# Out projection, feed-forward, norm and the second attention's first head joined without barriers, and the last feed-forward pair run piece by piece

## The chip, the cores and the metric

The kernel runs on one core of a Trainium2 chip. The metric is the device time of one execution in microseconds (us), lower is better. The times given are medians over runs.

## What is computed

One inference step of an encoder with two layers, for 1024 prompt tokens and 32 new ones, all in fp32. Layer 0 mixes tokens by sparse attention (a small indexer picks 256 keys per query), layer 1 by differential attention with 8 heads. Behind each mixer stand an out projection, a residual and a norm, and behind these the feed-forward part, a gated per-layer embedding and a second norm:

```python
    yp = layer_norm(ALPHA * yp + mp, ln_gain[i, 0], ln_bias[i, 0])     # mp = mixer's output @ w_out

def channel_and_ple(x, p, w13, w2, w_ple, w_gate, g, b):
    gate, up = jnp.split(x @ w13, 2, axis=-1)
    ffn = (jax.nn.silu(gate) * up) @ w2
    ple = jax.nn.sigmoid(x @ w_gate) * (p @ w_ple)
    return layer_norm(ALPHA * x + ffn + ple, g, b)
```

Model width is 1024, the feed-forward part's 2816, the embedding's 256. Outputs are the rows of both token sets after layer 1, and each layer's new keys and values.

## The kernel before

**Products.** An fp32 matrix is kept as two fp32r parts, high (rounded) and low (the rest), and a product is three matmuls: high by high, high by low, low by high. The tokens stand as columns: `x_hi` and `x_lo` hold the layer's input (128 partitions x 8 x 1056), `o_col` the running sum. The 1056 tokens are cut into three pieces of 352 for products with columns, or into nine tiles (eight of 128 and one of 32) for out projections and norms. A unit is a weight block of 8 x 128 x 128 (or 2 x 128 x 128 for the embedding), and its product with one piece is 24 matmuls of 352 columns (`unit_product`, `product`), in one PSUM bank.

**The ring.** SP loads a unit into `w_raw[s]` (`load_unit`, once the slot's previous unit is split), POOL splits it into `w_hi[s]` and `w_lo[s]` (`split_unit`, two operations, once TensorE has finished with the slot), TensorE waits for the split (`unit_ready`). There are four slots; `ring_plan` lists which slot each unit of a phase uses. A feed-forward pass uses 0, 1, 0, 1, 2, 3.

**Phases.** `program` runs ten: `load_x`, `index_projection`, `mixer_a`, `out_norm` A, `ffn` 0, `norm_tokens` 0, `attention_b`, `out_norm` B, `ffn` 1, `norm_tokens` 1. Each gives one function per engine. TensorE, ACT and DVE end every phase with a drain and wait for one another on `phase_over`; SP and POOL wait for that count only where a phase says so:

```python
                eng.drain().then_inc(c.phase_over, 1)
                eng.wait_ge(c.phase_over, 3 * n + 3)
```

Within a phase the order on each engine is the order in which its function is written; semaphores join them.

**`out_norm`** goes tile by tile. TensorE turns the mixer's output (B only, `turn_o`), multiplies it by the out weights (48 matmuls of 512 columns, line 1522) and, after six of the eight units, turns back the normalised rows of the tile before (`turn_back`). ACT makes `o_hi` (`o_high`, line 1537), DVE `o_lo` (line 1583). DVE adds the residual and takes statistics, ACT the root, DVE the coefficients, ACT the normalised rows `y_rows` (line 1566), and from the turned rows `x_new` (line 1574), which POOL splits into `x_hi` and `x_lo`. `o_hi` of tile t+1 is issued in the loop's turn of tile t, at its start.

**`ffn`** first loads p, turns it (line 1847) and splits it; then come eight columns of the gated embedding (a gate unit with sigmoid, a projection unit), and 11 passes of a hardware loop. Each pass, a *pair*, has two gate units, two up units, each for three pieces, silu and the product `h`, and then for each piece eight down products of 6 matmuls (line 1901), which DVE adds to `o_col` (line 1987).

**`norm_tokens`** turns `o_col` tile by tile into rows (line 1702), normalises them (root line 1736, rows line 1742), multiplies by the gain (POOL line 1692 in layer 0, DVE line 1760 in layer 1), adds the shift on POOL (line 1694) and stores them; in layer 0 it also turns them back and splits them (lines 1712, 1727, 1752). **`attention_b`** begins with the projections of its first head: V, K and Q units by three pieces each, with turns of V's and K's rows between.

Of the kernel before, what the change touches and what calls it, by code (L numbers as in the profile page):

```python
# [6 lines left out]
ALU = mybir.AluOpType  # L7
# [10 lines left out]
PIECES = 3  # L18
TP = TOK // PIECES
# [57 lines left out]
def ring_plan():  # L77

    phases = [("index", 1, [0, 1, 0, 1, 0]), ("attnA", 6, [0, 1]), ("outA", 1, [0, 1]),
              ("ple0", KC // 2, [0, 1, 2, 3]), ("ffn0", DFF // P // 2, [0, 1, 0, 1, 2, 3]),  # L80
              ("attnB", BH // 2, [0, 1, 0, 1, 0, 1]), ("outB", 1, [0, 1]),
              ("ple1", KC // 2, [0, 1, 2, 3]), ("ffn1", DFF // P // 2, [0, 1, 0, 1, 2, 3])]
    base, plan = [0] * 4, {}
    for name, passes, slots in phases:
        plan[name] = (tuple(base), slots)
        for s in range(4):
            base[s] += passes * slots.count(s)
# [82 lines left out]
def load_x(c):  # L170
# [27 lines left out]
    def pool(g):  # L198
# [793 lines left out]
def attention_b(c):  # L992
# [20 lines left out]
    squares = place("squares", [P, P], BF16)  # L1013
    assert at <= SAMPLE_OUT
# [10 lines left out]
    no = c.phase_no  # L1025
# [6 lines left out]
    FIRST_BANKS = (6, 0, 1, 2, 3, 6, 0, 1, 6)  # L1032
# [31 lines left out]

    def sync(sp):
        def weights(h, u):
            at = ((2 * D, D, 0)[u]) + P * h
            load_unit(c, sp, name, *unit(h, u), [(whole, w[:, :, at:at + P])], KC)

        for u in (V, K, Q):  # L1070
            weights(0, u)
        sp.wait_ge(c.phase_over, 3 * no)
        for h in range(BH):
# [6 lines left out]
            if h + 1 < BH:  # L1080
                weights(h + 1, V)
# [3 lines left out]
            if h + 1 < BH:  # L1085
                weights(h + 1, K)
# [3 lines left out]
            if h + 1 < BH:  # L1090
                weights(h + 1, Q)
# [16 lines left out]
    def tensor(pe):  # L1108
        def bank_read(h, n):
# [6 lines left out]
        def project(h, u, t):  # L1116
# [3 lines left out]
            before = [x for x in range(n) if piece_bank(h, x // 3, x % 3) == b]  # L1120
            if before:
                bank_read(h, before[-1])
            elif h >= 1:
                bank_read(h - 1, 8)
            last = unit_product(c, bank(c, b, TP), s, KC, c.x_hi, c.x_lo, t)
            piece_done(c, last, t, s_piece, s)

        def turn_rows(h, r):
            pe.wait_ge(s_col, 6 * h + (2, 3, 3, 5, 6, 6)[r])
            if 6 * h + r >= 1:  # L1130
                pe.wait_ge(s_rows, 6 * h + r)
            b = bank(c, ROWS)
            for j, t in enumerate(row_tiles(r)):
                cols = P if t < QT else NEW
                mm = nc.tensor.transpose(b[0:cols, P * j:P * j + P], col[:, P * t:P * t + cols], c.ident[:, :])
# [54 lines left out]
        for step in items(0):  # L1190
            for what in step:
                item(0, what)
# [13 lines left out]
    def scalar(act):  # L1206
        def project(h, u, t):
            i, v = unit(h, u)
            await_piece(c, act, name, i, v, t, s_piece, 3 * h + u)
# [57 lines left out]
        for step in items(0):  # L1267
            for what in step:
                item(0, what)
# [13 lines left out]
    def vector(v):  # L1283
        def project(h, u, t):
# [4 lines left out]
            if u == K:  # L1289
                v.wait_ge(s_col, 6 * h + 3 + t + 1)  # L1290
# [50 lines left out]

        v.wait_ge(s_iota, 2)
# [5 lines left out]
        for step in items(0):  # L1348
            for what in step:
                item(0, what)  # L1350
# [16 lines left out]
def out_norm(c, kind):  # L1367
# [87 lines left out]
    def pool(g):  # L1455
# [11 lines left out]
        for t in range(T):  # L1467
# [649 lines left out]
```

## Time and profile before

| what | us |
|---|---|
| median of 3 runs | 3404.48 (3397.68 to 3405.16) |
| profiled execution | 3402.7 |
| its span in the trace | 3400.9 |
| TensorE busy | 3134.8 (92%) |
| POOL, DVE, ACT busy | 1042.6, 1513.2, 887.1 |
| mean granted clock of TensorE | 0.952 of full |

All phases run one after the other on one core. Busy shares are over the whole span; the profile also gives them for any stretch, with the clock that was granted to TensorE in it (1.00 is full, 2.4 GHz). The chain that ended last leads back from the last instruction through whatever released each one. In a timeline row the bracket gives how long the engine was idle before and what ended that.

### The profile page before, as it was taken

The page shows a single profiled execution, that of the slowest core. Times are in us where ns is not written, and L with a number is a line of the kernel's source. Part 1 is how long each engine was busy: PE and PEld are TensorE (multiplying, and loading weights), DVE is VectorE, ACT ScalarE, POOL GpSimd, SP SyncE. Part 2 cuts the span into 40 slices and gives each one's busy share as a digit, 9 for nine tenths or more (in the row PEclk, how much of TensorE's full clock was granted, in tenths as well). Part 3 has the DMA queues.
Part 4 walks back from the last instruction along what each step waited for, and adds up shares of the span by engine and source line. Part 5 has one row for each costly group of instructions (what it writes and reads, how often), then busy time and mean ns, then how long its engine had stood idle before and what let it go on. Part 6 is the DMA issues. An engine that isn't in the chain of part 4 may idle for free.

```text
span 3400.9 us, 49928 instructions
## 1 busy us (share of the span) xinstructions
PE 3134.8 (92%) x19621; PEld 2921.1 (86%) x19621; DVE 1513.2 (44%) x2880; ACT 887.1 (26%) x1921; POOL 1042.6 (31%) x504
## 2 busy tenths in 40 slices
PE   7896999976999999999968999987889999999996
PEld 7586777764999999999967999976689999999996
DVE  2589764432434333432352555563334343334335
ACT  2355444423110111101122445453311101110112
POOL 2132000032443334333443222213244433443333
PEclk8998799988999999999988999998989999999997
DMA  2121000011211111111112111111021111111111
GB/s 82 32 51 51 1 1 1 1 56 36 65 45 62 37 43 43 55 44 43 44 47 68 55 41 46 47 39 56 21 75 50 44 56 37 44 48 56 37 49 51
DMA packets 209355, 149.48 MB, mean 44 GB/s; under 512 B 28914, under 2 KB 195764, under 8 KB 209236
## 3 DMA queue, kind: packets, MB, share of 16 engines
q1 hardware_dynamic: 209236, 147.85, 14.2%
q8 instruction: 80, 1.31, 0.2%
q14 instruction: 39, 0.32, 0.0%
HBM read 128.09 MB, written 19.73 MB: 43 GB/s over the span
## 4 chain that ended last, share of the span: by engine, by line
PE 84%; DVE 7%; ACT 3%; issue 2%; POOL 1%; DMA 1%; ACTq 0%; SPq 0%; POOLq 0%; DVEq 0%
PE psum L151 46%; PE psum L1901 15%; PE psum L1522 5%; PE psum L612 4%; PE psum L578 2%; PE psum L593 2%; DVE junk L827 2%; PE psum L1186 2%; PE psum L1160 2%; PE psum L1174 1%; PE psum L533 1%; PE psum L547 1%; ACT x_newA L1574 1%; DVE ln_part L1769 1%; ACT x_newB L1574 1%
## 5 line engine op out<-in xcount | busy, mean ns | idle before, releaser
L151 PE MATMUL psum<-x_hi,w_hi 128*128 128x352 f32 (+1 forms) x3192 | 1040.6, 326 | 29.5 <-POOL w_lo L122 13.8
L151 PE MATMUL psum<-x_lo,w_hi 128*128 128x352 f32 (+1 forms) x3192 | 1028.1, 322 | 0.0
L151 PE MATMUL psum<-x_hi,w_lo 128*128 128x352 f32 (+1 forms) x3192 | 1028.0, 322 | 0.0
L120 POOL TENSOR_TENSOR w_hi<-w_raw,zeros 128x1024 fp32r<-128x1024 f32 (+1 forms) x209 | 386.8, 1851 | 1615.4 <-PE psum L151 1359.2
L151 PEld LDWEIGHTS psum<-x_hi,w_hi 128*128 128x128 f32 (+1 forms) x3192 | 601.8, 189 | 31.6 <-issue 21.2
L151 PEld LDWEIGHTS psum<-x_lo,w_hi 128*128 128x128 f32 (+1 forms) x3192 | 602.9, 189 | 0.4
L151 PEld LDWEIGHTS psum<-x_hi,w_lo 128*128 128x128 f32 (+1 forms) x3192 | 601.6, 188 | 0.5
L122 POOL TENSOR_TENSOR w_lo<-w_raw,w_hi 128x1024 fp32r<-128x1024 f32 (+1 forms) x209 | 485.1, 2321 | 16.4
L1973 DVE TENSOR_TENSOR gate<-psum,gate 128x352 f32<-128x352 f32 x132 | 69.3, 525 | 830.5 <-PE psum L151 830.5
L1901 PE MATMUL psum<-h_hi,w_hi 128*128 128x352 f32 x1056 | 340.6, 323 | 0.0
L1901 PE MATMUL psum<-h_lo,w_hi 128*128 128x352 f32 x1056 | 338.3, 320 | 0.0
L1901 PE MATMUL psum<-h_hi,w_lo 128*128 128x352 f32 x1056 | 338.0, 320 | 0.0
L1987 DVE TENSOR_TENSOR o_col<-psum,o_col 128x352 f32<-128x352 f32 x528 | 263.4, 519 | 149.3 <-PE psum L1901 147.1
L1977 DVE TENSOR_TENSOR h_lo<-gate,h_hi 128x352 fp32r<-128x352 f32 x132 | 210.2, 1617 | 0.3
L1901 PEld LDWEIGHTS psum<-h_lo,w_hi 128*128 128x128 f32 x1056 | 198.4, 188 | 0.0
L1901 PEld LDWEIGHTS psum<-h_hi,w_hi 128*128 128x128 f32 x1056 | 198.0, 188 | 0.0
L1901 PEld LDWEIGHTS psum<-h_hi,w_lo 128*128 128x128 f32 x1056 | 197.9, 187 | 0.0
L1933 ACT ACTIVATE h_hi<-gate 128x352 fp32r<-128x352 f32 x132 | 65.8, 498 | 469.6 <-DVE gate L1973 469.6
L612 PEld LDWEIGHTS psum<-valsA,ptA 128*128 128x128 f32 (+1 forms) x1216 | 150.2, 194 | 37.6 <-issue 21.4
L612 PE MATMUL psum<-valsA,ptA 128*128 128x65 f32 (+1 forms) x1216 | 168.3, 283 | 0.9 <-ACT ptA L698 0.4
L1930 ACT ACT_TABLE_LOAD x22 | 28.2, 1283 | 532.7 <-PE psum L151 532.7
L1327 DVE CUSTOM_DVE_ANT_0 probB<-psum,distB 128x128 f32<-128x128 f32 (+5 forms) x144 | 96.4, 707 | 121.5 <-PE psum L1160 120.5
(458 smaller groups left out, 4166.9 us busy)
## 6 DMA issues: line engine op xcount, KB each, us to landing
w_raw<-in_ffn_w_dram SPq DMA_DIRECT2D x132, 512.0 KB
w_raw<-in_b_w_in_dram SPq DMA_DIRECT2D x24, 512.0 KB
w_raw<-in_ple_w_gate_dram SPq DMA_DIRECT2D x16, 512.0 KB
x_nat<-in_x_prompt_dram SPq DMA_DIRECT2D x8, 512.0 KB, 3.7
w_raw<-in_a_w_in_dram SPq DMA_DIRECT2D x8, 512.0 KB
w_raw<-in_a_w_in_dram SPq DMA_DIRECT2D x16, 256.0 KB
x_rows<-x_rows SPq DMA_DIRECT2D x8, 512.0 KB, 2.6
out_new_b_v_prompt_dram<-valsB SPq DMA_DIRECT2D x8, 512.0 KB, 3.4
```

The lines of the kernel that those rows point to most:

```text
L120: nc.gpsimd.tensor_tensor(c.w_hi[s][:, 0:kc], c.w_raw[s][:, 0:kc], zero, ALU.add).then_inc(c.split[s], 1)
L122: nc.gpsimd.tensor_tensor(c.w_lo[s][:, 0:kc], c.w_raw[s][:, 0:kc], c.w_hi[s][:, 0:kc].bitcast(F32), ALU.subtract).then_inc(c.split[s], 1)
L151: last = c.nc.tensor.matmul(out, w, x, start=(n == 0), stop=(n == 3 * len(terms) - 1))
L578: mm = nc.tensor.matmul(c.psum[0:n, 1024 * m + a:1024 * m + a + size], queries[rows, 4 * c2 + 2 * i + j, q:q + n], keys[rows, c2, key:key ...
L593: mm = nc.tensor.transpose(bank(c, 4 + k % 2)[0:size, P * x:P * x + n], prob[0:n, g % 3, m, key:key + size], c.ident[0:n, 0:n])
L612: mm = nc.tensor.matmul(c.psum[0:n, at:at + 65], pt[0:size, k, x, 0:n], vals[0:size, blk, 2 * c2 + m, :], start=(j == 0 and x == 0), stop= ...
L1327: nc.vector.tensor_tensor_reduce(prob[:, sl, m, 0:L], c.psum[:, 1024 * m:1024 * m + L], dist[:, o:o + L], slope(h), -LOWEST, ALU.add, ALU.min,
L1522: mm = nc.tensor.matmul(out, o[t % 2][:, u, 0:n], ww[:, cols], start=(j == 0 and x == 0), stop=(j == KC - 1 and x == 2))
L1901: mm = nc.tensor.matmul(o, w[s][:, m, :], h[:, j, piece(t)], start=(j == 0 and k == 0), stop=(j == 1 and k == 2))
L1973: nc.vector.tensor_tensor(gate[:, 1, piece(t)], bank(c, 3 + t, TP), gate[:, 0, piece(t)], ALU.mult).then_inc(s_h, 1)
L1977: nc.vector.tensor_tensor(h_lo[:, j, piece(done)], gate[:, 1, piece(done)], h_hi[:, j, piece(done)].bitcast(F32), ALU.subtract).then_inc(s ...
L1987: nc.vector.tensor_tensor(o, bank(c, (6 + m) % 8, TP), o, ALU.add).then_inc(s_da, 1)
```

## The change

1. **Ring.** Six slots; each of the six units of a feed-forward pair has its own. Slots 4 and 5 lie where p and its two parts lay, whose last use is before the first pair.
2. **Out projection.** `o_hi` and `o_lo` are issued two tiles ahead, from the turn of tile t for tile t+2. The last tile's turn back is given to the next phase.
3. **From out projection to feed-forward.** No barrier. SP loads the first two embedding units before p, POOL splits them in the out projection's loop after tile 6, TensorE runs the first gate unit's pieces 0 and 1 right after the last tile's product, then the last turn back, the turns of p, and piece 2.
4. **`ffn` and `norm_tokens` become `ffn_norm`.** The loop has 10 passes; the last pair is written out piece by piece, and the turns of the norm stand between its pieces. The gain is now multiplied on DVE in both layers.
5. **Norm and first head.** In layer 0 the norm's later tiles (turns of 5 to 8, turns back of 4 to 8) are issued between the V, K and Q pieces of `attention_b`'s first head. V's and K's weights are loaded and split before the third tile's shift.
6. Barriers stay behind `load_x`, `index_projection`, `mixer_a`, `attention_b` and at the end.

The core of the diff:

```diff
@@ ring_plan @@
-              ("ple0", KC // 2, [0, 1, 2, 3]), ("ffn0", DFF // P // 2, [0, 1, 0, 1, 2, 3]),
+              ("ple0", KC // 2, [0, 1, 2, 3]), ("ffn0", DFF // P // 2, [0, 1, 2, 3, 4, 5]),
@@ out_norm, pool @@
+            if t == T - 3:
+                c.ple_first[layer](g)
@@ out_norm, tensor @@
-        turn_back(T - 1)
@@ out_norm, scalar @@
-            if t >= 1 and t + 1 < T:
-                o_high(t + 1)
+            if t + 2 < T:
+                o_high(t + 2)
             act.wait_ge(s_mv, b_mv + t + 1)
@@ out_norm, vector: after the coefficients of tile t @@
-            if t >= 1 and t + 1 < T:
-                o_low(t + 1)
...
+            if t + 2 < T:
+                o_low(t + 2)
@@ ffn_norm, sync @@
+        ple_unit(sp, 0, 0)
+        ple_unit(sp, 0, 1)
+        sp.wait_ge(s_omm, b_o + T)
         sp.dma_start(p_nat[:, 0:QT, :], c.dram["p_prompt"][layer, 0].rearrange("(t p) n -> p t n", p=P)).then_inc(s_pn, 16)
@@ ffn_norm, pool @@
+        for u in range(6):
+            split_unit(c, g, fn, L, u, KC)
+        g.wait_ge(s_par, b_par + 32)
+        shifted(g, 0)
+        shifted(g, 1)
+        if not last_one:
+            split_unit(c, g, "attnB", 0, 0, KC)
+            split_unit(c, g, "attnB", 0, 1, KC)
+        for t in range(2, T):
+            shifted(g, t)
@@ ffn_norm, tensor @@
+        gate_input(0, 0)
+        gate_input(0, 1)
+        c.turn_back_last[layer](pe)
+        pe.wait_ge(s_oy, 2 * b_o + 2 * T)
+        turn_p()
+        gate_input(0, 2)
+        turn_p_sample()
...
+        gate_last(0, 0)
+        up_last(0, 0)
+        gate_last(1, 0)
+        up_last(1, 0)
+        gate_last(0, 1)
+        down_last(0)
+        turn_rows(pe, 0)
+        up_last(0, 1)
+        turn_rows(pe, 1)
+        gate_last(1, 1)
+        if not last_one:
+            turn_back(pe, 0)
+        up_last(1, 1)
+        if not last_one:
+            turn_back(pe, 1)
+        gate_last(0, 2)
+        down_last(1)
+        turn_rows(pe, 2)
+        up_last(0, 2)
+        turn_rows(pe, 3)
+        gate_last(1, 2)
+        if not last_one:
+            turn_back(pe, 2)
+        up_last(1, 2)
+        turn_rows(pe, 4)
+        if not last_one:
+            turn_back(pe, 3)
+        down_last(2)
+        if last_one:
+            for t in range(5, T):
+                turn_rows(pe, t)
@@ attention_b, tensor @@
+        late.turn(pe, 5)
+        late.turn(pe, 6)
+        late.back(pe, 4)
+        project(0, V, 0)
+        late.turn(pe, 7)
+        late.back(pe, 5)
+        project(0, K, 0)
+        late.back(pe, 6)
+        late.turn(pe, 8)
+        project(0, V, 1)
+        late.back(pe, 7)
+        project(0, K, 1)
+        late.back(pe, 8)
+        project(0, V, 2)
+        project(0, K, 2)
+        turn_rows(0, 0)
+        project(0, Q, 0)
...
@@ program @@
-        for make, *args in ((load_x,), (index_projection,), (mixer_a,), (out_norm, "A"),
-                            (ffn, 0), (norm_tokens, 0), (attention_b,), (out_norm, "B"), (ffn, 1),
-                            (norm_tokens, 1))[:LIMIT]:
+        for make, *args in ((load_x,), (index_projection,), (mixer_a,), (out_norm, "A"), (ffn_norm, 0), (attention_b,),
+                            (out_norm, "B"), (ffn_norm, 1))[:LIMIT]:
+            goes_on = make is out_norm or (make is ffn_norm and args[0] == 0)
```

The functions `turn_rows`, `stats`, `root`, `coefs`, `normal`, `gained`, `shifted`, `turn_back`, `high` and `low` of `ffn_norm` hold the same instructions as `norm_tokens` did, one tile each.

**ACT in the first out projection.** Here `o_hi0A` and `o_hi1A` are the two buffers of `o_hi`, the line with `ln_coefA` is the root, the one with `y_rows` the normalised rows. Before, from the last of the weights on:

```order
L1548 ACTIVATE far_hi5A<-w_raw 128x1024
L1564 ACT_TABLE_LOAD
L1564 ACTIVATE ln_coefA<-ln_mvA,eps 128x1
L1566 ACTIVATE y_rows0A<-y_rows0A,ln_coefA 128x1024
L1574 ACTIVATE x_newA<-psum,params 128x128 x8
L1537 ACTIVATE o_hi0A<-o_col 128x1024
L1564 ACTIVATE ln_coefA<-ln_mvA,eps 128x1
L1566 ACTIVATE y_rows1A<-y_rows1A,ln_coefA 128x1024
L1574 ACTIVATE x_newA<-psum,params 128x128 x8
L1537 ACTIVATE o_hi1A<-o_col 128x1024
```

And now:

```order
L1662 ACTIVATE far_hi5A<-w_raw 128x1024
L1651 ACTIVATE o_hi0A<-o_col 128x1024
L1678 ACT_TABLE_LOAD
L1678 ACTIVATE ln_coefA<-ln_mvA,eps 128x1
L1680 ACTIVATE y_rows0A<-y_rows0A,ln_coefA 128x1024
L1688 ACTIVATE x_newA<-psum,params 128x128 x8
L1651 ACTIVATE o_hi1A<-o_col 128x1024
L1678 ACTIVATE ln_coefA<-ln_mvA,eps 128x1
L1680 ACTIVATE y_rows1A<-y_rows1A,ln_coefA 128x1024
L1688 ACTIVATE x_newA<-psum,params 128x128 x8
```

`o_hi` of tile 2 stood behind `x_new` of tile 0 and now stands ahead of tile 0's root; so for every later tile.

**ACT in the last pair of layer 0.** From the silu of the second third's first gate (`gate_130`) on; L2194 is silu, L2198 makes `h_hi`, L1863 is the root, L1880 the normalised rows, L1897 `x_hi` of the next layer. None of the norm's rows stood here before:

```order
L2194 ACTIVATE gate_130<-psum 128x352
L1863 ACT_TABLE_LOAD
L1863 ACTIVATE ln_coef_138<-ln_mv_137,eps 128x1
L1880 ACTIVATE x_rows_0_131<-psum,ln_coef_138 128x1024
L2198 ACTIVATE h_hi_128<-gate_130 128x352
L1863 ACTIVATE ln_coef_138<-ln_mv_137,eps 128x1
L1880 ACTIVATE x_rows_0_132<-psum,ln_coef_138 128x1024
L2194 ACT_TABLE_LOAD
L2194 ACTIVATE gate_130<-psum 128x352
L1897 ACTIVATE x_hi<-psum 128x4x128 x2
```

The norm of tiles 0 and 1 now stands between two silus, with a table load on each side.

**POOL after the last pair of layer 0.** Before, the V and K splits (L120, L122) stood behind all nine gains (L1692) and shifts (L1694); the last rows of the norm and what followed were:

```order
L1692 TENSOR_TENSOR x_rows_0_127<-x_rows_0_127,gain_rows_128 32x1024
L1694 TENSOR_TENSOR x_rows_0_127<-x_rows_0_127,shift_rows_129 32x1024
L120 TENSOR_TENSOR w_hi<-w_raw,zeros 128x1024
L122 TENSOR_TENSOR w_lo<-w_raw,w_hi 128x1024
L120 TENSOR_TENSOR w_hi<-w_raw,zeros 128x1024
L122 TENSOR_TENSOR w_lo<-w_raw,w_hi 128x1024
L1099 IOTA distB 128x1024
```

And now (L1891 is the shift, L121 and L123 the split):

```order
L1891 TENSOR_TENSOR x_rows_0_131<-x_rows_0_131,shift_rows_135 128x1024
L1891 TENSOR_TENSOR x_rows_0_132<-x_rows_0_132,shift_rows_135 128x1024
L121 TENSOR_TENSOR w_hi<-w_raw,zeros 128x1024
L123 TENSOR_TENSOR w_lo<-w_raw,w_hi 128x1024
L121 TENSOR_TENSOR w_hi<-w_raw,zeros 128x1024
L123 TENSOR_TENSOR w_lo<-w_raw,w_hi 128x1024
L1891 TENSOR_TENSOR x_rows_0_133<-x_rows_0_133,shift_rows_135 128x1024
```

The gains are gone from POOL, and the two splits stand between the shifts of tiles 1 and 2.

## Rows read from the trace of the kernel before

**Rows 1.** The page: busy us by engine; the chain that ended last.

```profile
PE 3134.8 (92%) x19621; PEld 2921.1 (86%) x19621; DVE 1513.2 (44%) x2880; ACT 887.1 (26%) x1921; POOL 1042.6 (31%) x504
...
PE psum L151 46%; PE psum L1901 15%; PE psum L1522 5%; PE psum L612 4%; PE psum L578 2%; PE psum L593 2%; DVE junk L827 2%; PE psum L1186 2%; PE psum L1160 2%; PE psum L1174 1%; PE psum L533 1%; PE psum L547 1%; ACT x_newA L1574 1%; DVE ln_part L1769 1%; ACT x_newB L1574 1%
```

**Rows 2.** Busy time by stretch: us, PE, PEld, DVE, ACT, POOL busy (x count), PEclk, DMA, GB/s.

```profile
707.03:821.80 114.77, 92.48 (x394) 73.95 (x392) 34.97 (x57) 37.07 (x77) 33.00 (x14) 0.93 0.09 29
...
722.29:737.67 15.38, 12.08 (x57) 9.76 (x57) 5.00 (x9) 5.39 (x11) 5.16 (x3) 1.00 0.10 34
...
821.80:835.50 13.70, 13.70 (x56) 6.56 (x56) 2.87 (x7) 4.25 (x10) 2.20 (x1) 0.88 0.01 1
...
835.50:856.90 21.40, 4.66 (x27) 4.26 (x26) 6.88 (x12) 6.44 (x16) 9.90 (x7) 0.68 0.41 112
...
856.93:860.40 3.47, 3.47 (x13) 3.47 (x14) 0.00 (x0) 0.00 (x0) 3.31 (x4) 0.54 0.61 178
...
2332.02:2448.32 116.30, 97.31 (x441) 79.93 (x439) 35.62 (x69) 38.57 (x84) 26.67 (x13) 0.91 0.09 29
...
2460.50:2482.00 21.50, 5.07 (x27) 4.51 (x27) 6.99 (x12) 6.47 (x16) 9.95 (x7) 0.60 0.40 111
...
976.30:1733.60 757.30, 757.30 (x4752) 757.04 (x4752) 267.13 (x397) 77.72 (x143) 279.82 (x128) 1.00 0.14 43
...
1733.60:1839.75 106.15, 64.62 (x381) 60.36 (x380) 38.18 (x76) 29.07 (x51) 60.31 (x28) 0.79 0.23 77
...
3358.50:3400.90 42.40, 15.16 (x73) 11.61 (x72) 30.67 (x55) 14.77 (x19) 21.11 (x9) 0.59 0.26 103
```

**Rows 3.** Timeline, out projection tiles: start us, us, engine, line, tiles [idle before it].

```profile
751.41 1.09 ACT L1537 ACTIVATE o_hi0A<-o_col 128x1024 fp32r<-128x1024 f32 x1
...
752.53 2.07 DVE L1583 TENSOR_TENSOR o_lo0A<-o_col,o_hi0A 128x1024 fp32r<-128x1024 f32 x1 [11.56 <-ACT o_hi0A L1537]
...
754.66 0.69 PE L1522 MATMUL psum<-w_hi,o_hi0A 128*128 128x512 f32 x1 [3.29 <-DVE o_lo0A L1583]
...
765.65 2.90 ACT L1574 ACTIVATE x_newA<-psum,params 128x128 f32<-128x128 f32 x8 [6.41 <-PE psum L1501]
...
2407.68 1.03 PE L1501 MATMUL psum<-ident,y_rows0B 128*128 128x128 f32 x8
```

**Rows 4.** The chain of waits, second out projection: start us, us, what, count.

```profile
2332.02 8.21 PE psum L1522 x36
```

**Rows 5.** Timeline between first out projection and feed-forward phase.

```profile
841.41 1.06 PE L1501 MATMUL psum<-ident,y_rows0A 32*128 32x32 f32 x8 [5.89 <-ACT y_rows0A L1566]
...
844.90 0.39 SPq L1818 DMA_DIRECT2D p_nat<-in_p_prompt_dram  x1
...
850.88 3.34 PE L1847 MATMUL psum<-ident,p_nat 128*128 128x128 f32 x16 [8.41 <-DMA p_nat<-in_p_sample_dram]
```

**Rows 6.** Timeline of the first norm phase.

```profile
1734.30 1.97 PE L1702 MATMUL psum<-ident,o_col 128*128 128x128 f32 x16 [0.67 <-DVEq L2068]
...
1737.12 1.28 ACT L1736 ACT_TABLE_LOAD   x1 [25.12 <-DVE ln_mv L1773]
...
1739.13 1.20 ACT L1742 ACTIVATE x_rows<-psum,ln_coef 128x1024 f32<-128x1024 f32 x1 [0.42 <-DVE ln_coef L1777]
...
1741.10 1.74 DVE L1777 SCALAR_TENSOR_TENSOR ln_coef<-ln_mv,ln_coef 128x1 f32<-128x1 f32 x1
...
1742.90 2.34 POOL L1694 TENSOR_TENSOR x_rows<-x_rows,shift_rows 128x1024 f32<-128x1024 f32 x1
...
1747.31 1.08 ACT L1727 ACTIVATE x_hi<-psum 128x512 fp32r<-128x512 f32 x2 [0.80 <-PE psum L1712]
...
1748.42 1.29 DVE L1752 TENSOR_TENSOR x_lo<-psum,x_hi 128x512 fp32r<-128x512 f32 x2 [3.17 <-ACT x_hi L1727]
```

**Rows 7.** Timeline of the last norm phase.

```profile
3366.14 1.22 DVE L1760 TENSOR_TENSOR x_rows<-x_rows,gain_rows 128x1024 f32<-128x1024 f32 x1
...
3374.74 0.48 PE L1702 MATMUL psum<-ident,o_col 128*128 128x128 f32 x1 [1.61 <-ACT x_rows L1742]
```

More of the change, by code:

```diff
@@ L1347, in vector @@
         v.wait_ge(s_dist, 2)
-        for step in items(0):
-            for what in step:
-                item(0, what)
+        project(0, Q, 0)
+        rows(0, 3)
+        project(0, Q, 1)
+        rows(0, 4)
+        project(0, Q, 2)
+        rows(0, 5)
+        late.rows_stored(v)
         for g in range(STEPS + 2):
@@ new lines, in gained, with shifted, high @@
+    def gained(v, t):
+        n = rows(t)
+        v.wait_ge(s_n, b_n + t + 1)
+        nc.vector.tensor_tensor(xt[t % 3][0:n, :], xt[t % 3][0:n, :], gain[0:n, :], ALU.mult).then_inc(s_gn, 1)
+    def shifted(g, t):
+        n = rows(t)
+        g.wait_ge(s_gn, b_gn + t + 1)
+        nc.gpsimd.tensor_tensor(xt[t % 3][0:n, :], xt[t % 3][0:n, :], shift[0:n, :], ALU.add).then_inc(s_x, 1)
+    def high(act, t):
+        n = rows(t)
+        act.wait_ge(s_bt, t + 1)
+        for b in (0, 1):
+            ins = nc.scalar.activation(c.x_hi[:, 4 * b:4 * b + 4, tokens(t)],
+                                       bank(c, 4 + b).rearrange("p (k q) -> p k q", k=4)[:, :, 0:n], ACT.Copy)
+        ins.then_inc(s_hi, 1)
@@ new lines, in low, with rows_stored @@
+    def low(v, t):
+        n = rows(t)
+        v.wait_ge(s_hi, t + 1)
+        for b in (0, 1):
+            ins = nc.vector.tensor_tensor(c.x_lo[:, 4 * b:4 * b + 4, tokens(t)],
+                                          bank(c, 4 + b).rearrange("p (k q) -> p k q", k=4)[:, :, 0:n],
+                                          c.x_hi[:, 4 * b:4 * b + 4, tokens(t)].bitcast(F32), ALU.subtract)
+        ins.then_inc(s_lo, 1)
+    def rows_stored(eng):
+        for j in range(3):
+            eng.wait_ge(s_out[j], b_out + 48)
@@ new lines, in high_last @@
+        def high_last(j, t):
+            act.wait_ge(s_h, b_h + 3 + last_count(j, t))
+            nc.scalar.activation(h_hi[:, j, piece(t)], gate[:, 1, piece(t)], ACT.Copy).then_inc(s_hh, 1)
+        silu_last(0, 0)
+        high_last(0, 0)
+        silu_last(1, 0)
+        high_last(1, 0)
+        silu_last(0, 1)
+        root(act, 0)
+        normal(act, 0)
+        high_last(0, 1)
+        root(act, 1)
+        normal(act, 1)
+        silu_last(1, 1)
+        if not last_one:
+            high(act, 0)
```

832 lines of the change are left out of this document (534 added, 298 removed).

## The prediction

> **What bounds the kernel now.** I read the page first: TensorE is busy for 3134.8 us of the span of 3400.9, and the chain that ended last is made of its products, with single percents for DVE and ACT lines [rows 1]. So a change pays where TensorE waits or runs slowly, and the next view is busy time by stretch. The steady part needs no help: ten and a bit of the eleven feed-forward pairs show 757.30 us of TensorE in 757.30, at clock 1.00 [rows 2]. The change touches the other rows of that view: the two loops of the out projection (92.48 busy of 114.77, and 97.31 of 116.30), the stretches from an out projection to its feed-forward (21.40 and 21.50 us, with 4.66 and 5.07 busy), the first norm with the second attention's first head (64.62 of 106.15), and the last norm (15.16 of 42.40) [rows 2]. Their idle time and low clocks hold all that can be won. The timeline then tells what each wait is.
>
> Unit prices, all from rows: a matmul of 352 columns at full clock takes 757.30 / 4752 = 0.159 us, so a piece of 24 takes 3.82 and a down piece of 48 takes 7.63 [rows 2]; one of 512 takes 8.21 / 36 = 0.228 [rows 4]; eight transposes take 1.03 [rows 3]. A pair takes 12 pieces of 3.82 and three of 7.63, 68.7 us.
>
> **The change, part by part.** The sum is made against the profiled execution, 3402.7 us, which is 1.8 above its span and 1.8 below the median of the runs.
>
> *Out projection, loop.* Before each tile TensorE waits 3.29 us for o_lo, which DVE began at once when ACT's o_hi was there; o_hi stood behind the previous tile's x_new of 2.90 us on ACT's queue [rows 3]. The change issues o_hi and o_lo two tiles ahead, so both are done about a tile before use. They take 1.09 and 2.07 us [rows 3], and neither engine is full: ACT 37.07 and DVE 34.97 of 114.77 [rows 2]. What is late next is nothing: a tile's normalised rows are turned after six of eight units of the next tile's products, and I see no wait there. A tile then takes 48 x 0.228 + 1.03 = 11.98 us; its busy time was 12.08 in the one tile shown, at clock 1.00 [rows 2]. Seven tiles: 83.9 for 114.77, **-30.9**. The short last tile goes from 13.70 at clock 0.88 to 12.0, **-1.7** [rows 2]. In the second one a tile has another eight transposes: 13.0, so 91 for 116.30, **-25.3**.
>
> *From out projection to feed-forward.* Of 21.40 us TensorE works 4.66 [rows 2]. It waits 5.89 for the last tile's rows, then the barrier, then the DMAs of p, issued at 844.90, after which its transposes start at 850.88 [rows 5]. The change loads the first gate weights before p, splits them on POOL during tile 6, and puts two gate pieces (2 x 3.82) right behind the last product: they cover the 5.89. The DMA of p is issued when the last product ends, and had taken 850.88 - 844.90 = 6.0 us, less than the 7.6 of the pieces. What is left is 1.06 + 3.34 of transposes [rows 5], some 0.3 for p's sample, and 0.5 for odd waits, an estimate: 5.2 for 21.40, **-16.2**. The pieces themselves are only moved. At the old start 13 matmuls took 3.47 us at clock 0.54, where 13 x 0.159 = 2.07 [rows 2]; without the idle stretch ahead that goes: **-1.7** with its neighbours. The second boundary: 21.50 to 5.2, and the same 1.7, **-18.0**.
>
> *Six-slot ring.* Each of the six units of a pair has its own slot. POOL's work stays the same (279.82 us for 64 units, 4.37 each, in 757.30) [rows 2], TensorE had no wait there, so **0**. Its cover is that a unit's split is needed a pair later; the last rival says what it costs if that goes.
>
> *Last pair of layer 0, norm, first head.* Before: 68.7, and 106.15 to the first logits [rows 2]: 174.8. After, the pair is cut by pieces, and the turns of tiles 0 to 4 and back-turns of 0 to 3 stand between them. Pair 68.7, nine groups of transposes 9.3. Waits: a tile's chain from the end of its turn (1734.30, of which half the 16, so 1735.3) over the table load of 1.28 to the end of its normalised rows (1739.13 + 1.20) is 5.0 us [rows 6]. The next turn needs this tile's bank and comes behind one piece of 3.82, so it waits 1.2, at tiles 1 and 3; 0.7 ahead of tiles 0 and 2, as for the first turn now [rows 6], for the last add. POOL splits V and K weights (two units, 8.7 us) between the shifts of tiles 1 and 2. K's slot comes free after the second up piece of the last third; 4.37 of split and 2.34 of shift [rows 6] make 6.7 us, the back-turn of tile 2 comes 1.2 + 1.03 + 3.82 = 6.0 later: 0.7. A DVE operation on one element lasted 1.74 us there and ended as POOL's did [rows 6]; for such holdings I add 1.8 to that wait and 1.2 at the adds. Together 7.5 of waits, pair 85.5. From there nine groups of transposes (9.3), nine pieces (34.4), row turns (2.6), 46.3, and 0.7 first. The waits here stand on chains with no piece of the right length beside them: a back-turn is followed by x_hi 1.08 and x_lo 1.29 [rows 6], before which a product may not start. I take 8, from 9 back-turn chains of which most have a piece in between. Bounds: 0 if all is covered, and 25 if each of nine tiles shows its 1.08 + 1.29 plus 0.4. Total 140.5 for 174.8, **-34.3**, within -42 and -17.
>
> Moved past on the queues: SP issues gain, shift and the V and K loads ahead of the stores of the rows, Q's among them; V and K wait for slots whose own splits the pair's first pieces have needed. On POOL, Q's split (4.37) waits for V's last piece and runs against K's last piece and a row turn, 3.82 + 0.5: even, 0. The stores end beside products, the iotas too.
>
> DVE now multiplies by gain in layer 0 too, 1.22 us a tile [rows 7], POOL only shifts: in stretches where TensorE's pieces are the longer path, 0.
>
> A table load cost 1.28 us here, and the normalised rows, with the root and two DVE operations in between, began 0.73 us after its end (1738.40 to 1739.13) [rows 6]. *ScalarE: Activation LUTs* of the Trainium skill, section "What ACT_TABLE_LOAD costs", puts a switch at about 2.66 us, a drain included. Behind this load the trace has no room for one. By the page the four switches in the open, at tiles 0 and 2 of both layers, would each add 1.4, and the sum would end 5.5 us higher.
>
> *Last norm.* Five of nine turns go into the last pair: 5.1 of transposes and 5.4 of waits by the same chain, 10.5 more there. What is left runs as before from tile 5's turn at 3374.74 to the end at 3400.9, 26.2 us [rows 7]. 42.40 becomes 36.6, **-5.8**.
>
> Sum: 30.9 + 1.7 + 17.9 + 25.3 + 18.0 + 34.3 + 5.8 = 133.9. 3402.7 - 133.9 = 3268.8, and with 1.8 to the median **3271 us**.
>
> **Rivals.**
> 1. *The clock falls among the turns.* For: the stretch with the norm has mean clock 0.79, those at the boundaries 0.68 and 0.60, the last norm 0.59 [rows 2], each with waits and transposes. Against: the tile from 722.29 ran eight transposes in its twelve busy microseconds at 1.00 after waits of 3.3 us [rows 2, 3]. If the late part (55 us) and 30 us of the two last pairs run at 0.8, that adds 85 x 0.25, 21 less some waiting it hides: about 16, 3287. The Trainium skill's *TensorE: Matmul & The Clock Gate*, "Part 4: PE-mode transpose", says that a transpose does not count as PE-busy in the same way; by it the fall would come wherever turns stand close together, which is this rival. The tile at 1.00 speaks against it only where products surround the turns.
> 2. *Longer chains.* ACT and DVE run one written order through pieces, norm and splits; each waits for the other and for POOL, and one late operation shifts all. If half the 34.3 and the 5.8 is lost: +20, 3291.
> 3. *The out projection has another bound.* The chain product, add, statistics, root, rows, turn, x_new, POOL's split might need more than a tile. At 15 us a tile the 14 full tiles give back 14 x 2.5 to 3.0, 40: 3311. Against: no engine but TensorE has over a third of that stretch [rows 2].
> 4. *The ring turns serial, slower.* Had the order of slots been wrong, so that POOL may split a unit only when the pair ahead has ended, each of 20 steady pairs would show a split of 4.37 and a load of 512 KB, at the 178 GB/s of [rows 2] 2.9 us: 7.3 us, 146 in all, 3417. It decides from 6.7 us a pair. Against: the first slot is free after 11.4 us of a pair of 68.7, and the last two are wanted 45.8 us into the next.
> 5. *The work joined does nothing*, since the waits come back at the first product that needs the same data: about 3400. The rows name causes that the change does remove, so little for this.
>
> **How the numbers follow.** The forecast has 0.66, on its own 3254 to 3285 (-8 and +17 in the head, and a few for each boundary). Rival 1 has 0.13, rival 2 0.10, rival 3 0.05, rival 4 0.03, rival 5 0.03. The range 3252 to 3304 takes in the first two rivals and leaves out the others and both tails, under 2 in 10. A change of 0.2% is 6.8 us, about what a measurement can tell. Faster by more: 0.66 + 0.13 + 0.10 + 0.05, and half of rival 5, 0.95; same 0.02; slower 0.03.
>
> **What would show it.** In the profile after: tiles of 12.0 and 13.0 us in the out projections, with o_hi ahead of the root and no wait for o_lo; about 5 us of TensorE time outside products between last tile and gate, clock near 1.00 at its first pieces; 68.7 us for a steady pair, with no wait for a split; the last pair of layer 0 at about 85 us, waits of about 1.2 us at the turns of tiles 1 and 3; first logits 140 us after the last pair's start. I am wrong if a tile takes over 13.5 us, if TensorE waits in a steady pair, or if the granted clock of the last pair or the first head falls below 0.9.

## The result and the profile after

The changed kernel takes 3288.4 us (median of 4 runs, 3282.6 to 3293.85) where the kernel before takes 3404.6 beside it; the ratio is 0.9666 (95% interval 0.9655 to 0.9678). That is 116 us less. The forecast was 3271, 134 less, with a range of 3252 to 3304.

The page of the changed kernel, busy time and the chain that ended last, answering to [rows 1] (L152 is the product, L2033 the down product, L1637 the out projection):

```profile
PE 3108.2 (94%) x19621; PEld 2902.7 (88%) x19621; DVE 1554.4 (47%) x2889; ACT 887.2 (27%) x1921; POOL 1021.8 (31%) x495
...
PE psum L152 48%; PE psum L2033 15%; PE psum L1637 6%; PE psum L613 5%; PE psum L579 3%; PE psum L594 3%; DVE junk L828 2%; PE psum L1225 2%; PE psum L1199 2%; PE psum L1213 1%; PE psum L534 1%; PE psum L548 1%; PE psum L1174 0%; PE psum L1591 0%; DMA x_nat<-in_x_prompt_dram 0%
```

Busy time by stretch, columns as in [rows 2]. The ten rows are: seven tiles of the first out projection, its last tile, the way through the third gate piece, the wait at the feed-forward part, ten pairs, the last pair, the rest of the norm with the first head to its first logits, seven tiles of the second out projection, the second boundary, and the last norm.

```profile
711.72:794.50 82.78, 82.78 (x393) 69.15 (x394) 35.31 (x56) 35.62 (x70) 25.77 (x12) 1.00 0.12 39
797.40:809.21 11.81, 11.81 (x57) 6.16 (x56) 4.08 (x7) 4.31 (x11) 9.86 (x6) 1.00 0.11 34
809.21:827.36 18.15, 16.11 (x100) 15.38 (x98) 6.65 (x11) 8.04 (x18) 11.29 (x9) 0.91 0.50 137
930.60:942.41 11.81, 0.21 (x2) 0.00 (x0) 11.58 (x7) 0.00 (x0) 11.65 (x6) 0.70 0.31 89
942.41:1630.85 688.44, 688.44 (x4321) 688.44 (x4322) 244.77 (x359) 70.64 (x130) 256.17 (x119) 1.00 0.15 44
1630.85:1716.20 85.35, 79.72 (x505) 77.51 (x504) 42.08 (x75) 23.84 (x35) 29.92 (x13) 0.98 0.06 26
1716.20:1774.50 58.30, 49.03 (x309) 46.72 (x309) 25.26 (x43) 16.53 (x33) 20.25 (x11) 0.94 0.25 77
2263.21:2352.27 89.06, 89.06 (x449) 74.60 (x450) 43.37 (x69) 36.45 (x76) 25.76 (x12) 1.00 0.11 36
2366.98:2383.57 16.59, 14.54 (x100) 13.82 (x98) 6.65 (x11) 8.04 (x18) 9.86 (x6) 1.00 0.51 145
3263.43:3292.07 28.64, 5.51 (x33) 4.05 (x32) 16.48 (x25) 5.69 (x8) 9.35 (x4) 0.62 0.20 78
```

TensorE works through both loops without a wait, at full clock, and a pair takes 68.84 us, as was said. One row was in no term of the sum: 11.8 us in which TensorE does nothing, in front of the first feed-forward product. To see what each part gave, both traces are cut at the same products (start times of matmuls, in us):

| stretch | before | after | difference | forecast |
|---|---|---|---|---|
| start to first out product of layer 0 | 688.3 | 697.4 | +9.1 | 0 |
| first to last product, out projection, layer 0 | 146.9 | 111.4 | -35.4 | -32.6 |
| to the last embedding product | 138.1 | 121.7 | -16.4 | -17.9 |
| to the first feed-forward product | 3.0 | 11.9 | **+8.9** | 0 |
| to the first logits of the second attention | 863.5 | 832.0 | -31.4 | -34.3 |
| to the first out product of layer 1 | 477.6 | 477.5 | -0.1 | 0 |
| first to last product, out projection, layer 1 | 142.8 | 114.6 | -28.1 | -25.3 |
| to the last embedding product | 138.2 | 120.1 | -18.1 | -18.0 |
| to the first feed-forward product | 3.0 | 11.9 | **+8.9** | 0 |
| to the end | 799.6 | 793.5 | -6.2 | -5.8 |

The first row is code that the change does not touch. Over the fourteen traces of this study it lies between 684.6 and 697.4. Without it the difference is -117.9, and the forecast's -133.9 with the two new waits added is -116.1.

The timeline of the changed kernel ahead of that product, DVE, POOL and TensorE (start us, us; the bracket is the idle time before and its end):

```profile
932.81 0.51 DVE L2267 TENSOR_TENSOR gate<-psum,gate 128x352 f32<-128x352 f32 x1
933.36 1.67 DVE L2270 SCALAR_TENSOR_TENSOR o_col<-x_lo,gate 128x352 f32<-128x352 f32 x1
934.72 2.50 POOL L123 TENSOR_TENSOR w_lo<-w_raw,w_hi 128x1024 fp32r<-128x1024 f32 x1
935.06 2.54 DVE L2273 SCALAR_TENSOR_TENSOR o_col<-x_hi,o_col 128x352 f32<-128x352 f32 x1
937.18 2.17 POOL L121 TENSOR_TENSOR w_hi<-w_raw,zeros 128x1024 fp32r<-128x1024 f32 x1
937.52 0.51 DVE L2267 TENSOR_TENSOR gate<-psum,gate 128x352 f32<-128x352 f32 x1
938.07 1.67 DVE L2270 SCALAR_TENSOR_TENSOR o_col<-x_lo,gate 128x352 f32<-128x352 f32 x1
939.43 2.50 POOL L123 TENSOR_TENSOR w_lo<-w_raw,w_hi 128x1024 fp32r<-128x1024 f32 x1
939.77 2.55 DVE L2273 SCALAR_TENSOR_TENSOR o_col<-x_hi,o_col 128x352 f32<-128x352 f32 x1
942.41 0.66 PE L152 MATMUL psum<-x_hi,w_hi 128*128 128x352 f32 x1 [11.60 <-ACTq L2176]
```

A piece's three DVE operations take 4.7 us, and the two with both inputs in SBUF end just after an operation of POOL; the one with an input in PSUM takes 0.51 beside POOL all the same. POOL is splitting the first pair's third unit and those behind it, which in four slots could not start before the pair did: in the trace of the kernel before, POOL's last split ahead of the pair ends at 965.74, DVE's last nine operations come from 971.76 on, and each lasts 0.52 or 0.53. And the signal that TensorE waited for is ACT's, which the change had moved behind DVE's last addition. The theory: the six slots let POOL into DVE's way, and the moved signals put the whole DVE chain in front of TensorE. By opening signals I mean the `sem_inc` calls with which ACT and DVE say, before the first pair, that its banks and buffers are free; in the kernel before both gave them ahead of the embedding's loop.

### The profile page after: what moved, and what is told of

Its sections match the earlier page's. It is cut to its first block, busy times and chain, and to the rows that moved or that the text cites. A ratio compares the mean times of both kernels' runs of the same rounds, so it can differ in the third digit from the quotient of the medians.

```text
span 3292.1 us, 49272 instructions
## 1 busy us (share of the span) xinstructions
PE 3108.2 (94%) x19621; PEld 2902.7 (88%) x19621; DVE 1554.4 (47%) x2889; ACT 887.2 (27%) x1921; POOL 1021.8 (31%) x495
## 4 chain that ended last, share of the span: by engine, by line
PE 88%; DVE 6%; issue 2%; ACT 2%; POOL 1%; DMA 1%; POOLq 0%; SPq 0%; ACTq 0%; DVEq 0%
PE psum L152 48%; PE psum L2033 15%; PE psum L1637 6%; PE psum L613 5%; PE psum L579 3%; PE psum L594 3%; DVE junk L828 2%; PE psum L1225 2%; PE psum L1199 2%; PE psum L1213 1%; PE psum L534 1%; PE psum L548 1%; PE psum L1174 0%; PE psum L1591 0%; DMA x_nat<-in_x_prompt_dram 0%
## 5 line engine op out<-in xcount | busy, mean ns | idle before, releaser
L152 PE MATMUL psum<-x_hi,w_hi 128*128 128x352 f32 (+1 forms) x3192 | 1041.4, 326 | 40.1 <-ACTq L2176 23.2
L152 PE MATMUL psum<-x_lo,w_hi 128*128 128x352 f32 (+1 forms) x3192 | 1028.0, 322 | 0.0
L152 PE MATMUL psum<-x_hi,w_lo 128*128 128x352 f32 (+1 forms) x3192 | 1027.9, 322 | 0.0
L121 POOL TENSOR_TENSOR w_hi<-w_raw,zeros 128x1024 fp32r<-128x1024 f32 (+1 forms) x209 | 381.9, 1827 | 1549.6 <-PE psum L152 957.8
L152 PEld LDWEIGHTS psum<-x_hi,w_hi 128*128 128x128 f32 (+1 forms) x3192 | 601.7, 189 | 42.8 <-ACTq L2176 23.8
L152 PEld LDWEIGHTS psum<-x_lo,w_hi 128*128 128x128 f32 (+1 forms) x3192 | 602.8, 189 | 0.5
L152 PEld LDWEIGHTS psum<-x_hi,w_lo 128*128 128x128 f32 (+1 forms) x3192 | 601.5, 188 | 0.5
L123 POOL TENSOR_TENSOR w_lo<-w_raw,w_hi 128x1024 fp32r<-128x1024 f32 (+1 forms) x209 | 491.8, 2353 | 16.4
L2033 PE MATMUL psum<-h_hi,w_hi 128*128 128x352 f32 x1056 | 340.8, 323 | 1.3 <-DVE h_lo L2308 1.0
L2033 PE MATMUL psum<-h_lo,w_hi 128*128 128x352 f32 x1056 | 338.3, 320 | 0.0
L2033 PE MATMUL psum<-h_hi,w_lo 128*128 128x352 f32 x1056 | 338.1, 320 | 0.0
L2033 PEld LDWEIGHTS psum<-h_hi,w_hi 128*128 128x128 f32 x1056 | 198.0, 188 | 2.0 <-issue 1.6
L2033 PEld LDWEIGHTS psum<-h_lo,w_hi 128*128 128x128 f32 x1056 | 198.3, 188 | 0.0
L2033 PEld LDWEIGHTS psum<-h_hi,w_lo 128*128 128x128 f32 x1056 | 197.9, 187 | 0.0
L2290 DVE TENSOR_TENSOR h_lo<-gate,h_hi 128x352 fp32r<-128x352 f32 x120 | 197.3, 1670 | 0.0
```

The costliest lines, as they stand in the source:

```text
L121: nc.gpsimd.tensor_tensor(c.w_hi[s][:, 0:kc], c.w_raw[s][:, 0:kc], zero, ALU.add).then_inc(c.split[s], 1)
L123: nc.gpsimd.tensor_tensor(c.w_lo[s][:, 0:kc], c.w_raw[s][:, 0:kc], c.w_hi[s][:, 0:kc].bitcast(F32), ALU.subtract).then_inc(c.split[s], 1)
L152: last = c.nc.tensor.matmul(out, w, x, start=(n == 0), stop=(n == 3 * len(terms) - 1))
L2033: mm = nc.tensor.matmul(o, w[s][:, m, :], h[:, j, piece(t)], start=(j == 0 and k == 0), stop=(j == 1 and k == 2))
L2290: nc.vector.tensor_tensor(h_lo[:, j, piece(done)], gate[:, 1, piece(done)], h_hi[:, j, piece(done)].bitcast(F32), ALU.subtract).then_inc(s ...
```

## The experiments

Times are medians beside runs of the kernel before on the same chip. "Wait" is the stretch from the last embedding product to the first feed-forward product in the run's trace (layer 0, layer 1), where the changed kernel has 11.9 and 11.9 and the kernel before 3.0 and 3.0.

### The wait in front of the feed-forward part

**ACT's signal early.**

```diff
+        act.sem_inc(s_si, 3)
         for x in range(4):
             p_high(x)
...
         act.wait_ge(s_acc, b_acc + 3 * KC)
-        act.sem_inc(s_si, 3)
```

> The changed kernel with one line moved: ACT gives its three opening signals for the feed-forward gates (s_si) before the embedding part, as the kernel before did, and no longer after DVE's last addition. Theory: the wait of 11.60 us at the first feed-forward product of each layer is for that signal; without it TensorE waits only for DVE's last gate multiply, which ended at 938.03 where the product started at 942.41, so the wait becomes about 7.5 us, 4 less in each layer, 8 us less in all. Rival (the wait has another cause, such as a split that comes late): the wait stays at 11.6 and the time stays.

3285.1 us, ratio 0.9658 (0.9645 to 0.9672); waits 10.0 and 9.6. The wait now ends with a signal of DVE (9.7 us, DVEq L2277), for which the change has the same order: its opening `sem_inc` calls stand behind the last addition too. So only 2 us went in each layer, half of what was expected, and the median's 3 us lie inside the interval. ACT's signal was the last of several, not the only one.

**POOL held back.**

```diff
         with g.Fori(0, L) as i:
             for u in range(6):
+                if u == 2:
+                    g.wait_ge(s_acc, b_acc + 3 * KC)
                 split_unit(c, g, fn, i, u, KC)
```

> The changed kernel with one wait added: POOL splits the third unit of the first feed-forward pair only after DVE's last addition of the embedding part. Theory: with six slots POOL splits units 2 to 5 just while DVE adds the last three pieces, and DVE's operations last 2.55 and 1.67 us in place of 0.53 because of that. Held back, they last 0.53, the last addition ends 3.6 us after the last embedding product as in the kernel before, and the wait falls from 11.6 to about 3.8 us: 7.8 less in each layer, 15.6 in all; the third unit is needed 22.9 us later, so nothing new waits. Rival (DVE's operations are long for another reason, such as the unrolled form of the instructions or the DMAs): they stay at 2.55 us and the time stays, or it gets longer by a wait for a split.

3268.1 us, ratio 0.9617 (0.9603 to 0.9630), clear of the changed kernel's interval; waits 3.4 and 3.3, 17 us less together where 15.6 were expected. The same rows in its trace:

```profile
921.31 0.52 DVE L2269 TENSOR_TENSOR gate<-psum,gate 128x352 f32<-128x352 f32 x1
921.86 0.52 DVE L2272 SCALAR_TENSOR_TENSOR o_col<-x_lo,gate 128x352 f32<-128x352 f32 x1
922.41 0.52 DVE L2275 SCALAR_TENSOR_TENSOR o_col<-x_hi,o_col 128x352 f32<-128x352 f32 x1
923.19 1.89 POOL L121 TENSOR_TENSOR w_hi<-w_raw,zeros 128x1024 fp32r<-128x1024 f32 x1 [10.94 <-DVE o_col L2275]
923.12 0.56 PE L152 MATMUL psum<-x_hi,w_hi 128*128 128x352 f32 x1 [3.05 <-DVEq L2279]
```

Every DVE operation is back at 0.52. POOL stood idle for 10.9 us and nobody missed it. One wait on POOL gives back nearly all that the step cost in the two layers.

**Both edits.**

> Both edits of signal_early and pool_held in the changed kernel. Theory: the wait at the first feed-forward product is again 2.7 us as in the kernel before, 8.9 less in each layer, 17.8 us less than the changed kernel in all, about 3271. Rival: neither helps or only one of the two.

3273.9 us, ratio 0.9615 (0.9600 to 0.9630); waits 3.4 and 3.0. Beside the held POOL the early signal gives at most 0.3 us.

**The ring alone, in the kernel before** (its feed-forward units on slots 0 to 5, two slots added over p, and one wait on SP so that it loads them only when p has been turned). The run was made twice.

```diff
-... ("ffn0", DFF // P // 2, [0, 1, 0, 1, 2, 3]),
+... ("ffn0", DFF // P // 2, [0, 1, 2, 3, 4, 5]),
```

> The kernel before with the six-slot ring alone. Theory: the steady pairs stay at 68.7 us, and POOL's splits of units 2 to 5 fall on DVE's last additions of the embedding part; TensorE's wait at the first feed-forward product, which there ends with DVE's last gate multiply, grows from 2.70 to about 7.5 us, so the kernel becomes about 10 us slower than before. What I had put in the prediction for the ring, nothing: 3404 and a wait of 2.7 us.

> The kernel of ring_six a second time, since its median was 19 us above before and its trace accounts for 10. Theory (only the two waits): 10 us slower than before. Rival: 19 us again.

3420.9 us, ratio 1.0057 (1.0043 to 1.0070), and in the second set 3416.4, ratio 1.0035 (1.0021 to 1.0050): slower, by under 1%. The waits are 8.0 and 8.0 in both traces, 10 us together, and the steady pairs are unchanged. 12 to 19 us were measured. What is beyond the 10 is not explained: both traces are of executions at the low end of their sets (3412.1 and 3412.0), and there the second out projection takes 147.1 and 147.0 us where the kernel before has 142.8, and earlier stretches take as much less.

```profile
974.14 2.50 POOL L122 TENSOR_TENSOR w_lo<-w_raw,w_hi 128x1024 fp32r<-128x1024 f32 x1
974.57 2.46 DVE L1964 SCALAR_TENSOR_TENSOR o_col<-x_hi,o_col  x1
...
977.92 0.66 PE L151 MATMUL psum<-x_hi,w_hi 128*128 128x352 f32 x1 [7.68 <-DVE gate L1957]
```

**The ring with POOL held**, in the kernel before (the wait of the second experiment added).

> The kernel before with the six-slot ring, and POOL's split of the third unit of the first pair held until DVE's last addition of the embedding part. Theory: POOL's splits beside DVE's last additions are all that the ring costs; held back, the wait at the first feed-forward product is 3.0 us again and the time that of the kernel before, within 0.2%. Rival (the ring costs something else too, since ring_six was 19 us slower and its trace shows 10 of them in the two waits): 8 to 10 us slower than before.

The ratio is 1.0013 (0.9999 to 1.0027), no difference that can be told; the plain medians are 9 us apart (3411.5 and 3402.4), and its trace has 7.5 of them in the untouched part ahead of the first out projection. That the ring costs a little more than its overlap is not excluded. The waits are 3.0 and 3.0, and the one at the product ends as before:

```profile
985.30 0.42 PE L151 MATMUL psum<-x_hi,w_hi 128*128 128x352 f32 x1 [2.69 <-DVE gate L1959]
```

So of the 8.9 us at each feed-forward part some 5 are the ring's overlap alone (ring_six), and about 2 are ACT's signal behind DVE's last addition, made long by the same overlap (signal_early). The last 2 are left by difference and put down to DVE's signal, which ends the wait in signal_early; no run moves that one, so its share is argued and not measured.

### The terms that held

**The out projection's part alone, in the kernel before.**

```diff
-            if t >= 1 and t + 1 < T:
-                o_high(t + 1)
+            if t + 2 < T:
+                o_high(t + 2)
...
+            if t + 2 < T:
+                o_low(t + 2)
```

> The kernel before with the out projection's part of the change alone: o_hi and o_lo are issued two tiles ahead. Theory: from the first to the last product of an out projection 146.9 and 142.8 us become 111.4 and 114.6, as in the changed kernel, since TensorE's wait for o_lo (3.29 us a tile) and the low clock behind it were the only causes; nothing else changes, so 63.6 us less, about 3338. Rival (the other parts of the change helped the loop, or the wait turns into one for the rows to be turned back): a tile stays over 12.5 us and less than 50 us are won.

3337.9 us, ratio 0.9817 (0.9801 to 0.9832). First to last product: 113.1 and 114.2. Seven tiles in its trace, TensorE busy for all of it at full clock:

```profile
714.35:796.17 81.82, 81.82 (x386) 65.16 (x386) 35.34 (x55) 36.17 (x76) 30.06 (x14) 1.00 0.13 41
```

Two statements moved by one tile are worth 64 us, over half of the whole change.

**Turn back first.** The last tile's turn back is put ahead of the two gate pieces.

```diff
+        c.turn_back_last[layer](pe)
         gate_input(0, 0)
         gate_input(0, 1)
-        c.turn_back_last[layer](pe)
```

> The changed kernel with the last tile's turn back put ahead of the first two gate pieces of the embedding part instead of behind them. Theory: the pieces cover the chain of the last tile's normalised rows; in front of them TensorE waits some 5.9 us for these rows, as in the kernel before, and gets back the 2.0 us that it now waits for x_lo ahead of the third piece: 3.9 more at each of two boundaries, 7.8 us slower than the changed kernel. Rival (the chain is hidden anyway): no difference.

3300.4 us, ratio 0.9697 (0.9684 to 0.9710), 12 us slower than the changed kernel. The wait is back:

```profile
803.92 1.05 PE L1591 MATMUL psum<-ident,y_rows0A 32*128 32x32 f32 x8 [5.90 <-ACT y_rows0A L1680]
```

The stretches to the last embedding product grow by 4.6 and 6.6 us, 11 where 7.8 were expected (the 4.6 is small because the changed kernel's own trace has a low clock there in layer 0, see below). The products behind the open wait begin at a lower clock, 0.67 in the first 8 us, which I had left out:

```profile
803.92:812.00 8.08, 8.08 (x40) 8.02 (x40) 0.00 (x0) 2.26 (x8) 4.35 (x4) 0.67 0.48 116
```

### The last pair and the first head

**K's split later**, in the kernel of pool_held.

```diff
             split_unit(c, g, "attnB", 0, 0, KC)
-            split_unit(c, g, "attnB", 0, 1, KC)
         for t in range(2, T):
             shifted(g, t)
+            if t == 3 and not last_one:
+                split_unit(c, g, "attnB", 0, 1, KC)
```

> The kernel of pool_held with POOL's split of K's weights moved from between the shifts of tiles 1 and 2 to behind the shift of tile 3. Theory: TensorE's wait of 3.24 us at the turn back of tile 2 is for a shift that stands behind this split (5.1 us long there), and it goes: 3 us less than pool_held, unless it comes back at K's first piece. Rival (the shift of tile 2 is late because DVE's gain and h_lo last 2.6 us each beside POOL): the wait stays at half or more, and the time changes by less than 1.5 us.

3261.9 us, ratio 0.9595 (0.9579 to 0.9611). The rows of the changed kernel that it answers to:

```profile
1693.10 3.23 POOL L123 TENSOR_TENSOR w_lo<-w_raw,w_hi 128x1024 fp32r<-128x1024 f32 x1
1696.29 2.62 POOL L1891 TENSOR_TENSOR x_rows<-x_rows,shift_rows 128x1024 f32<-128x1024 f32 x1
1698.97 1.13 PE L1846 MATMUL psum<-ident,x_rows 128*128 128x128 f32 x8 [3.24 <-POOL x_rows L1891]
```

And in held_k's trace the same turn back, with no wait:

```profile
1680.17 1.03 PE L1846 MATMUL psum<-ident,x_rows 128*128 128x128 f32 x8
```

The stretch to the first logits is 826.1 us for 829.0 in pool_held: 2.9 less, as expected.

**Late norm tiles in one block.** TensorE, ACT and DVE do tiles 5 to 8 of the norm first, and then V, K and Q; here TensorE's part:

```diff
         late.back(pe, 4)
-        project(0, V, 0)
         late.turn(pe, 7)
         late.back(pe, 5)
-        project(0, K, 0)
         late.back(pe, 6)
         late.turn(pe, 8)
-        project(0, V, 1)
         late.back(pe, 7)
-        project(0, K, 1)
         late.back(pe, 8)
+        project(0, V, 0)
+        project(0, K, 0)
+        project(0, V, 1)
+        project(0, K, 1)
         project(0, V, 2)
```

> The changed kernel with the late norm tiles (5 to 8) put ahead of all pieces of the second attention's first head on TensorE, ACT and DVE, not between them; no barrier comes back. Theory: the interleaving itself hides the norm's chains (in the kernel before one tile took 4.7 to 6.1 us there); four pieces, 15.3 us, no longer stand beside four tiles' chains, so the stretch from the first feed-forward product to the first logits grows from 832.0 us by about 10, between 6 and 15. Rival (only the missing barrier and the early splits brought the gain there): it grows by less than 3 us.

3301.6 us, ratio 0.9705 (0.9692 to 0.9719); the stretch to the first logits is 849.4, 17.3 more, over the expected 6 to 15. Busy time of the block by itself:

```profile
1707.90:1745.00 37.10, 20.39 (x104) 18.22 (x105) 19.78 (x34) 10.81 (x19) 10.56 (x6) 0.63 0.28 92
```

It had waits of up to 5.3 us and mean clock 0.63, where the interleaved stretch has 0.94. The interleaving pays twice, in waits and in clock.

**The changed kernel and the fastest version side by side.**

> The changed kernel itself, beside the next one on the same chip: 3288, 0.966 of before.

> The fastest version so far (POOL held at the start of the feed-forward part, K's split behind the shift of tile 3) beside the changed kernel: by the terms measured 17 and 3 us faster than the changed kernel, 0.9595 of before.

3288.5 us, ratio 0.9655 (0.9632 to 0.9678), and 3259.2 us, ratio 0.9572 (0.9548 to 0.9596). The version with POOL held and K's split later beats both kernels: 29 us less than the changed one by medians, 22.4 by the two traces without the untouched first part, of which 17 are the waits and 4 the stretch to the first logits. 17 and 3 were expected.

## Why the prediction held, and where it missed

The direction, the range and the order of the terms held; the single number was 17 us too low, and 3288.4 lies outside the 3254 to 3285 that the forecast was given on its own. The range held by the room that it left for rivals 1 and 2, which stand for other causes: that part is luck.

- **Out projection, loop.** A tile of 11.98 and one of 13.0 us were forecast; seven tiles of layer 0 take 82.8 and of layer 1 89.1, a little less. The run of that part alone shows that nothing else was needed, and rival 3 (15 us a tile) falls.
- **From out projection to feed-forward.** 5.2 us outside pieces were forecast. From the first gate product (809.05) to the third piece (821.50) lie 12.45, less 7.64 of pieces 4.8, of which 2.0 were a wait for x_lo that I had put at 0.5; the turns of p, at full clock, took 1.97 and not the 3.34 of [rows 5], which made up for it. The cover by the pieces is shown by back_first. What the sum left out is the clock behind that wait of 2.0 us: in layer 0, 11 matmuls of the third piece start 0.293 us apart where 0.159 is the price, 1.5 us in all, and that is why this row gave 16.4 for 17.9. In layer 1 and in the trace of changed_again they run at the full rate and the stretch is 120.1 and 120.2 us.
- **Six-slot ring: the step that failed.** It said that POOL's work stays the same and that TensorE had no wait there, and put 0. True of the pairs (688.44 of 688.44 busy), and ring_six shows 5 us a layer in front of them. I looked at whom the splits serve and not at whom they run beside: with free slots POOL starts early, into DVE's last additions. The row for that price was in the prediction, the DVE operation of 1.74 us that ended as POOL's did [rows 6], used there for the norm alone. The other half of the step is one that I did not list: the opening signals of ACT and DVE moved behind the last addition. Together they cost 8.9 us a layer, 17.8 us, and the term should have been +17.8 in place of 0; held POOL gives back 17.2 of it.
- **Last pair, norm, first head.** 140.5 us were forecast, 85.35 + 58.30 = 143.65 came. The pair was right to 0.2, by luck, since two errors cancel. Its waits were 5.6 us for 7.5: those at the turns of tiles 1 and 3 did not come, since the table load was placed right behind the silu ahead and not on the chain, and the one for tile 2 behind K's split was 3.2 for 2.5. Its busy time was 79.7 for 78.0: the 24 products right behind that wait took 5.4 us for 3.82. In the head the waits were 9.3 for 8.7 and the busy time 49.0 for 46.3, at mean clock 0.94. So most of what is missing here is clock. The second trace of the same kernel, changed_again, has 1.8 us less in this stretch.
- **Last norm.** 7.6 us more in the pair (76.3 for 68.7) and 28.6 behind it, for 10.5 and 26.2: near the same sum, 36.2 for 36.7, with one part too high and the other too low.
- **Rivals.** The measured time is near what rivals 1 and 2 give, 3287 and 3291, and neither is the reason. Rival 1 happened in small: the clock is 0.98 in the last pair and 0.94 behind it, and TensorE's busy time in the two is 4.4 us over the price at full clock, where the rival has 16, the last pair of layer 1 included, whose clock is 1.00. By the sentence on transposes in the Trainium skill's *TensorE: Matmul & The Clock Gate*, "Part 4: PE-mode transpose", the fall should come where turns stand close together, and among products little of it came; in late_serial, where turns and waits stand without products, the clock is 0.63, and whether turns or idle time do it these runs do not separate. Rival 2 (half of two terms lost) lost 3 us of the first, by the clock, and none of the second. Rival 4 (a serial ring) falls with the busy pairs.
- **Slips in the working.** The 4752 matmuls in 757.30 us are all eleven pairs, 432 each, and not "ten and a bit". Rival 3 at 15 us a tile loses 3.0 a tile in the first out projection but 2.0 in the second, 35 us and 3306. And the +17 in the head would end the forecast's own spread at 3288 and not 3285. None of them moves the forecast.

## What to carry to other kernels

More buffers let a producer run earlier, and here the price was paid by the engine that worked beside it at that moment: after such a change look at the engine next to it, at the seams between stages, and not only at the one that waits for the buffer. An opening signal belongs ahead of the work that it does not depend on, on each engine that gives one. Where a loop waits for an operand that an idle engine could have made a tile ago, two moved statements can be worth more than all fused stages.

## What the hardware showed

DVE operations with two inputs in SBUF last 0.52 us alone and 1.67 to 2.55 us in the rows above while POOL splits, each ending about 0.4 us after the end of a POOL operation (932.47 + 2.17 = 934.64, and 933.36 + 1.67 = 935.03); those with one input in PSUM keep their 0.51. POOL's two operations get longer too: 2.17 and 2.50 us there, 1.90 and 2.39 behind DVE's last addition in pool_held (at 927.50 and 929.47). The Trainium skill's *SBUF — State Buffer*, section "SBUF: two separate sides", has this as an exclusive lock between GpSimd and a DVE operation with two SBUF inputs, held for a whole instruction. The rows agree, and so does pool_held, where POOL is idle and every DVE operation lasts 0.52 or 0.53.

In these rows a switch of ACT's table costs the load and nothing else. Three rows of ACT in the changed kernel's last pair, back to back:

```profile
1667.51 1.21 ACT L1880 ACTIVATE x_rows<-psum,ln_coef 128x1024 f32<-128x1024 f32 x1 [0.52 <-DVE ln_coef L1870]
1668.74 1.28 ACT L2194 ACT_TABLE_LOAD   x1
1670.03 0.46 ACT L2194 ACTIVATE gate<-psum 128x352 f32<-128x352 f32 x1
```

The load stands 0.02 us behind the operation ahead and 0.01 us ahead of the silu. The Trainium skill's *ScalarE: Activation LUTs*, "What ACT_TABLE_LOAD costs", has about 2.66 us for a switch, a drain included. The load's own 1.28 us agrees, the drain does not show between these rows; the measurement decides.

What stays open: why the part ahead of the first out projection, which no edit touched, takes 685 to 697 us from trace to trace; the 2 to 9 us of ring_six beyond its two waits; and what DVE's opening signals, moved back alone, would give.
